# Layer B: one set of exponentials for two matrices, and 16x16 instead of 8x8 base blocks solved on VectorE

## What is computed

```python
    gc = jnp.cumsum(to_chunks(g, C, N), axis=-1)
    diff = gc[..., :, None] - gc[..., None, :]
    decay = jnp.where(tri, jnp.exp(jnp.where(tri, diff, 0.0)), 0.0)
    kb = kc * bc[..., None]
    lmat = jnp.where(strict, jnp.einsum('nbhik,nbhjk->nbhij', kb, kc) * decay, 0.0)
    rhs = jnp.concatenate([vc * bc[..., None], kb * jnp.exp(gc)[..., None]], axis=-1)
    sol = lax.linalg.triangular_solve(lmat, rhs, left_side=True, lower=True, unit_diagonal=True)
    u, w = sol[..., :dv], sol[..., dv:]
    aqk = jnp.einsum('nbhik,nbhjk->nbhij', qc, kc) * decay
    def step(S, xs):
        v_new = u_i - jnp.einsum('bhck,bhkv->bhcv', w_i, S)
        o_i = jnp.einsum('bhck,bhkv->bhcv', qg_i, S) + jnp.einsum('bhij,bhjv->bhiv', aqk_i, v_new)
        S = S * jnp.exp(gl_i)[..., None, None] + jnp.einsum('bhck,bhcv->bhkv', kdec_i, v_new)
```

## Time and profile before

| | us |
|---|---|
| median of three runs | 2143.05 |
| the three runs | 2143.21, 2138.21, 2143.05 |
| the profiled execution, whole | 2141.25 |
| its span, first to last instruction | 2139.2 |
| busy in the span: PE / DVE / ACT / POOL | 2098.6 / 954.5 / 711.9 / 449.6 |
| layer B's stage, on PE | 1062 to about 1701 |

### The profile page before, as it was taken

One profiled execution on the slowest core, in us unless ns is written; L12 is line 12 of the kernel. 1 busy time (PEld: TensorE's weight loads), 2 busy tenths in 40 slices (PEclk: granted clock), 3 DMA queues, 4 the chain that ended last, 5 costly groups with the idle time before them and its releaser, 6 DMA issues.

```text
span 2139.2 us, 39670 instructions
## 1 busy us (share of the span) xinstructions
PE 2098.6 (98%) x16046; PEld 1503.8 (70%) x16046; DVE 954.5 (45%) x2457; ACT 711.9 (33%) x1681; POOL 449.6 (21%) x640
## 2 busy tenths in 40 slices
PE   8999999999999999999999999999999999999998
PEld 6888888888888877555466676767766666665444
DVE  5234353354445445332255666666666233332252
ACT  4121311311231231221145555555555344542101
POOL 0522232231223214100033223322331200020000
PEclk9999999999999999999999999999999999999999
DMA  7511301211230137668212222222210361124451
GB/s 223 167 42 44 106 23 50 80 40 42 58 92 23 50 106 263 212 204 259 72 38 80 84 77 88 84 85 76 72 48 13 106 257 56 40 94 131 138 166 50
DMA packets 210251, 210.53 MB, mean 98 GB/s; under 512 B 14262, under 2 KB 181654, under 8 KB 209151
## 3 DMA queue, kind: packets, MB, share of 16 engines
q1 hardware_dynamic: 198070, 148.27, 23.4%
q0 software_dynamic: 12000, 59.73, 7.3%
HBM read 179.56 MB, written 68.23 MB: 116 GB/s over the span
## 4 chain that ended last, share of the span: by engine, by line
PE 48%; ACT 1%; DVE 1%; issue 0%; DVEq 0%
PE bank L2103 18%; PE bank L2913 8%; PE bank L3403 7%; PE bank L2161 5%; PE bank L2177 2%; PE bank L2159 2%; PE bank L2169 1%; PE bank L2929 1%; PE bank L2938 1%; PE bank L3381 1%; PE bank L3414 0%; PE bank L2192 0%; PE bank L3310 0%; PE bank L3287 0%; PE bank L2921 0%; PE bank L3297 0%
## 5 line engine op out<-in xcount | busy, mean ns | idle before, releaser
L887 PE MATMUL bank<-arena 128*128 128x256 f32 (+1 forms) x2688 | 631.7, 386 | 0.0
L887 PEld LDWEIGHTS bank<-arena 128*128 128x128 f32 x2688 | 494.5, 190 | 75.3
L2103 PE MATMUL bank<-arena 128*128 128x352 f32 x1296 | 457.7, 470 | 1.2 <-issue 1.1
L2103 PEld LDWEIGHTS bank<-arena 128*128 128x128 f32 x1296 | 217.9, 191 | 66.0 <-ACT arena L2338 0.6
L2913 PE MATMUL bank<-arena 128*128 128x352 f32 x576 | 176.4, 459 | 0.0
L3403 PE MATMUL bank<-arena 128*128 128x512 f32 x360 | 167.5, 599 | 0.0
L2161 PEld LDWEIGHTS bank<-arena 128*128 128x128 f32 x864 | 127.6, 194 | 44.2 <-DVE arena L2648 4.1
L2913 PEld LDWEIGHTS bank<-arena 128*128 128x128 f32 x576 | 106.6, 190 | 53.3
L1341 POOL TENSOR_TENSOR arena<-arena 128x272 f32<-128x272 f32 (+1 forms) x48 | 31.5, 656 | 507.7 <-ACT arena L1061 487.8
L2161 PE MATMUL bank<-arena 128*128 128x128 f32 x864 | 133.3, 280 | 4.0 <-DVE arena L2648 3.1
L1323 POOL TENSOR_TENSOR arena<-arena 128x512 f32<-128x512 f32 x96 | 122.7, 1278 | 11.1 <-POOL arena L1323 0.9
(11 more groups left out here) (433 smaller groups left out, 2800.4 us busy)
## 6 DMA issues: line engine op xcount, KB each, us to landing
arena<-in_w_in_a SPq DMA_DIRECT2D x48, 512.0 KB, 5.1
arena<-in_w_in_b SPq DMA_DIRECT2D x40, 512.0 KB, 6.6
arena<-in_cache_win_k SPq DMA_DIRECT2D x48, 256.0 KB, 6.1
arena<-in_cache_win_v SPq DMA_DIRECT2D x48, 256.0 KB, 4.8
out<-arena SPq DMA_DIRECT2D x40, 256.0 KB, 3.4
arena<-in_w_mem_kv SPq DMA_DIRECT2D x16, 512.0 KB, 8.1
arena<-in_cache_mem_k SPq DMA_DIRECT2D x32, 256.0 KB, 4.4
arena<-in_cache_mem_v SPq DMA_DIRECT2D x32, 256.0 KB, 4.2
```

The source lines that it names most:

```text
L887: m = nc.tensor.matmul(o[:, 0:hi - lo], w, y, start=k == 0 and i in (0, 1, 3, 5), stop=k == KH - 1, skip_group_check=i in (2, 4, 6))
L2103: m = nc.tensor.matmul(bank[j % 3][:, 0:PART], ring.slots[:, (B1 + b) % RING, k, :], part_in(k, part_), start=k == 0, stop=k == KD - 1)
```

## The change

Three things change.

1. A diagonal similarity. Row scaling by beta and by k's inverse norm on both sides is replaced by one column scaling, beta times the squared inverse norm, which is put in the exponent's bias. Then lmat and aqk hold the same exponentials: `ra` is broadcast and exponentiated once per group and multiplied with `kk` into LT and with `qk` into AT. `rl` and four of eight Exp go. The factors that come with v, k and the state change to suit (v times k's norm, k decayed times beta and the squared inverse norm); `factors` has four small DVE instructions with one wait on itself in place of three.
2. BASE is 16. Level 3 (x3, z3) goes from PE and DVE; DVE does 15 steps in place of 7 on 2 x 15 down to 2 x 1 entries per chunk (8 x j elements a partition in place of 16 x j), and the spreading transpose has 1920 columns in place of 896. `base_rows` waits for POOL's spread of the group before.
3. The slots: `ra` 5, `kt` 7, `kk` 8, `qk` 9, exps 7, choice 9, `base_rows` 11; steps 1, 1, 2, 1 in 12 to 15 and 2, 2, 1, 2, 1, 2 in 0 to 5; the norms in 1 to 5; x4 stays in slot 6. AT gets three buffers, LT two, in the spare branch rows of the last head.

The core of the diff (renamings of slices, `head_terms` and the prelude's three lines left out):

```diff
-FIRST_LEVEL = 3
+FIRST_LEVEL = 4
 BASE = 1 << FIRST_LEVEL
...
-    PREP = {6: ("kt",), 9: ("ra", "rl"), 11: ("qk", "kk"), 15: ("vt",)}
-    NEXT = ("rl", "kk")
-    LEVEL_SLOTS = {(3, "x"): 4, (3, "z"): 5, (4, "x"): 6, (4, "z"): 7, (5, "x"): 10, (5, "z"): 12, (6, "x"): 13, (6, "z"): 14}
-    AT_ROWS = 13
-    STEPS_BEFORE = {14: 1, 15: 1}
-    STEPS = {0: 1, 1: 2, 2: 1, 3: 1}
+    PREP = {5: ("ra",), 7: ("kt",), 8: ("kk",), 9: ("qk",), 15: ("vt",)}
+    NEXT = ("ra", "kk", "qk")
+    LEVEL_SLOTS = {(4, "x"): 6, (4, "z"): 7, (5, "x"): 10, (5, "z"): 12, (6, "x"): 13, (6, "z"): 14}
+    AT_ROWS = 11
+    STEPS_BEFORE = {12: 1, 13: 1, 14: 2, 15: 1}
+    STEPS = {0: 2, 1: 2, 2: 1, 3: 2, 4: 1, 5: 2}
...
-    AT_EXPS, AT_CHOICE = 9, 11
-    AT_SS, AT_ROOTS, AT_INV, AT_LOGS, AT_FACTORS, AT_OT = 3, 4, 5, 6, 7, 8
+    AT_EXPS, AT_CHOICE = 7, 9
+    AT_SS, AT_ROOTS, AT_INV, AT_LOGS, AT_FACTORS, AT_OT = 1, 2, 3, 4, 5, 8
...
-    TAP_AT = {0: 0, 4: 1, 11: 2}
-    conv_at = {1: (0, 1), 3: (0, 2), 4: (0, 3), 5: (1, 1), 7: (1, 2), 8: (1, 3), 12: (2, 1), 14: (2, 2), 15: (2, 3)}
+    TAP_AT = {0: 0, 6: 1, 11: 2}
+    conv_at = {1: (0, 1), 3: (0, 2), 4: (0, 3), 7: (1, 1), 9: (1, 2), 10: (1, 3), 12: (2, 1), 13: (2, 2), 15: (2, 3)}
...
-        def exps(G, name, buf, lo):
+        def exps(G):
...
-            readout(act, G, name)
+            readout(act, G, "ra")
+            act.wait_ge(hdv, 3 * G + 2)
             for n, c in enumerate(range(*GR[G % 2])):
-                i = nc.scalar.activation(buf[:, lo + n, :], buf[:, lo + n, :], ACT.Exp,
+                i = nc.scalar.activation(ATs[G % 3][:, n, :], ATs[G % 3][:, n, :], ACT.Exp,
                                          bias=hd[:, G // 2 % 2, BI, c:c + 1])
...
-            nc.vector.tensor_tensor(w[:, BI:RW + 1, :], w[:, LK:LK + 1, :].to_broadcast([P, 2, 4]), both_of(to_logs),
-                                    ALU.add).then_inc(hdv, 1)
-            nc.vector.tensor_tensor(w[:, NC_:KD_ + 1, :], w[:, RK:RK + 1, :].to_broadcast([P, 2, 4]),
-                                    both_of(to_roots), ALU.mult)
+            nc.vector.scalar_tensor_tensor(out=w[:, BI, :], in0=w[:, LK, :], scalar=2.0, in1=f(to_logs),
+                                           op0=ALU.mult, op1=ALU.add).then_inc(hdv, 1)
+            own(nc.vector.tensor_tensor(w[:, KD_, :], w[:, RK, :], w[:, RK, :], ALU.mult))
+            nc.vector.tensor_tensor(w[:, KD_, :], w[:, KD_, :], f(to_decays), ALU.mult)
             nc.vector.tensor_scalar(w[:, RQ, :], w[:, RQ, :], SCALE, None, ALU.mult).then_inc(hdv, 1)
...
-            if name == "rl":
-                nc.vector.tensor_tensor(lt, bk(b), wide4(mat(M_GT)), ALU.add).then_inc(rd_dve, 1)
-            elif name == "ra":
-                nc.vector.tensor_tensor(AT[:, cs, :], bk(b), wide4(mat(M_GE)), ALU.add).then_inc(rd_dve, 1)
+            if name == "ra":
+                nc.vector.tensor_tensor(at_, bk(b), wide4(mat(M_GE)), ALU.add).then_inc(rd_dve, 1)
             elif name == "kk":
-                dve.wait_ge(exd, 2 * G + 1)
-                nc.vector.tensor_tensor(lt, lt, bk(b), ALU.mult).then_inc(rd_dve, 1)
+                dve.wait_ge(exd, G + 1)
+                nc.vector.tensor_tensor(lt, at_, bk(b), ALU.mult).then_inc(rd_dve, 1)
...
             dve.wait_ge(chosen, 4 * (G + 1))
+            if G:
+                dve.wait_ge(spread, G)
```

More of the change, by code:

```diff
@@ L1905, in build @@
     spread_rows = upper[:, 2176:2176 + 4 * (BASE - 1) * 32]
-    LTs = [LT, upper[:, 3072:3584].rearrange("p (c e) -> p c e", e=P)]
-    to_logs, to_roots = (v.rearrange("p (t n) -> p t n", t=2)
-                         for v in (upper[:, 3584:3584 + 128], sb[:, small_at + 384:small_at + 512]))
+    spare = brT[:, HB - 1, 0:1024].rearrange("p (i c e) -> p i c e", i=2, e=P)
+    LTs = [LT, spare[:, 0]]
+    ATs = [AT[:, 0:4, :], AT[:, 4:8, :], spare[:, 1]]
+    to_logs, to_decays, minus_eg = (sb[:, small_at + 304 + 64 * i:small_at + 368 + 64 * i] for i in range(3))
     junk_s, junk_p = take(P), take(1)
@@ L1979, in build @@
     reader_of = lambda n: "act" if n == "ss" or n[:2] in ("qs", "tr") else "dve"
-    work = [(0, "ss"), (0, "rl"), (0, "kk")]
+    work = [(0, "ss"), (0, "ra"), (0, "kk"), (0, "qk")]
     for G in range(NG_ + 1):
@@ L2021, in build @@
     hcols = lambda v, h: v[:, h:64:HB]
-    RQ, RK, LK, NC_, KD_, BI, RW, SO = range(8)
+    RQ, RK, LK, QN, KN, KD_, BI, SO = range(8)
     def sides(v, k, b):
@@ L2211, in chunk_step @@
                 readout(pe, g, f"tr{c}")
-                to(g, f"av{c}", [(AT[:, c, :], vn[:, c % 2, :])])
+                to(g, f"av{c}", [(ATs[g % 3][:, cl, :], vn[:, c % 2, :])])
                 to(g, f"su{c}", [(kdec[:, c, :], vn[:, c % 2, :])])
@@ L2284, in _ @@
             unit(*u)
-        turned(0, "rl")
+        turned(0, "ra")
         for u in units[PER_HEAD + KD:PER_HEAD + 2 * KD]:
@@ L2288, in _ @@
         turned(0, "kk")
+        turned(0, "qk")
         for u in units[PER_HEAD + 2 * KD:PER_HEAD + AHEAD]:
@@ L2445, in _ @@
         silu(1, 0)
-        exps(0, "rl", LT, 0)
+        exps(0)
         piece(*second)
@@ L2463, in _ @@
                     chunk_step(G - 1, s)
[L2464 to L2467, removed]
+                if s == AT_EXPS and G + 1 < NG_:
+                    exps(G + 1)
                 if G == NG_ and s == 15:
@@ L2514, in norm_inverses @@
             h, cs = group(g)
-            w = hd[:, h % 2, RQ:RQ + 2, cs]
+            w = hd[:, h % 2, :, cs]
             readout(dve, g, "ss")
-            nc.vector.reciprocal(w, w).then_inc(hdv, 1)
+            nc.vector.reciprocal(w[:, RQ:RK + 1, :], w[:, QN:KN + 1, :]).then_inc(hdv, 1)
         def factors(g):
@@ L2522, in factors @@
             w = hd[:, h % 2, :, cs]
[L2523 removed]
+            f = lambda v: hcols(v, h)[:, cs]
             dve.wait_ge(hda, g + 1)
             dve.wait_ge(hdv, 3 * g + 1)
[L2526 to L2529 removed]
+            nc.vector.scalar_tensor_tensor(out=w[:, BI, :], in0=w[:, LK, :], scalar=2.0, in1=f(to_logs),
+                                           op0=ALU.mult, op1=ALU.add).then_inc(hdv, 1)
+            own(nc.vector.tensor_tensor(w[:, KD_, :], w[:, RK, :], w[:, RK, :], ALU.mult))
+            nc.vector.tensor_tensor(w[:, KD_, :], w[:, KD_, :], f(to_decays), ALU.mult)
             nc.vector.tensor_scalar(w[:, RQ, :], w[:, RQ, :], SCALE, None, ALU.mult).then_inc(hdv, 1)
         def head_terms():
[L2534 to L2538 removed]
+            nc.vector.tensor_tensor(to_logs, lbeta[:, 0:64], gc[:, 0:64], ALU.subtract)
+            nc.vector.tensor_tensor(to_decays, beta[:, 0:64], ekd[:, 0:64], ALU.mult)
+            own(nc.vector.tensor_scalar(minus_eg, eg[:, 0:64], -1.0, None, ALU.mult))
         def out_factors(g):
```

18 lines of the change are left out of this document (6 added, 12 removed).

## The result

| | median us | runs, lowest to highest |
|---|---|---|
| before | 2140.55 | 9, 2137.25 to 2143.26 |
| after | 2147.21 | 9, 2145.33 to 2149.24 |

The ratio is 1.0032, with a 95% interval of 1.0023 to 1.0041: the changed kernel is 6.7 us slower, and the prediction of 2137 missed by 10, with the wrong sign. The time lies within the range of 2118 to 2154. The profiled execution took 2148.14 us, its span is 2146.2. The page's busy times follow (us, share of the span, instructions): PE is busy 21.3 us less than before, and its share of the span fell from 98 to 97%.

What follows compares the result with a forecast made beforehand. PE, busy 98% of the span, was taken as the bound: 31.4 us gross gain less 26.7 (waits 21.5, start 2.2, end 3) made 4.7 faster, given as 2137. The range of 8 in 10 ran from 2118 to 2154.

Steps and rivals of the forecast that it cites:

- What PE loses, 1.89 a group: PE's list per group: z3 0.86, x3 0.57 and four `rl` transposes 0.46 go; times 16 is 30.2 us.
- DVE's durations: Step pairs at 0.0017 an element and 0.41 fixed, spread of 1920 columns 2.16; DVE carries 4.2 us more a group.
- x4's wait, 1.3: PE in slot 6 waits 1.3 us a group for DVE's factors, last two steps and transpose; bounds 0.9 and 2.0.
- x6's wait, 0.35: PE in slot 13 waits 0.35 us a group for DVE's spread and z5's readouts; bounds 0 and 0.8.
- DVE's free time between slot 14 and slot 2 takes up the rest: DVE has 1 to 2 us to spare before slot 2's readouts; POOL can take it away.
- Start and end, 2.2 and 3: Losses: 2.2 us at the start for the first base blocks, 3 from group 13 on, where DVE's chain sets the time.
- Rival A: DVE's chain is shorter than counted, x4 waits 0.4 at most: 21 us gain, 2120; chance 0.22.
- Rival B: x4's wait is 1.6 and half the groups drop PE's clock, decisive from about 1.5 on: 2153; chance 0.20.
- this trace agrees for the longer of its waits: In the kernel before, PE's clock fell after a wait of 1.54 us and stayed up after 1.37.
- Rival C: Each wait is 0.4 longer, POOL holding DVE in slot 5 or ACT late; no clock falls: 2142; chance 0.15.
- D: DVE is late in all slots from 11 to 5, steps costing more than the line; 1 us a group, 2150; chance 0.07.
- their own rule: No change lies between 2136.6 and 2149.5; forecast half faster: faster 0.42, no change 0.36, slower 0.22.

Runs made afterwards that it cites:

- e6: Changed kernel with the norms' sums behind slot 1's chunk product, last two steps in slot 4, slot 10's conv in slot 12: 2113.03 us, ratio 0.9866.
- e9: e6 with four projection units moved from the very end of the stage into slots 12 to 15 of group 13: 2108.86 us, ratio 0.9854.
- e4: Kernel before with the similarity (shared exponentials) alone, keeping BASE 8, level 3 and its slots: 2134.54 us, ratio 0.9981.
- e5: Kernel before with 16x16 base blocks alone, keeping both sets of exponentials and the norms in slots 3 to 7: 2138.85 us, ratio 0.9993.
- e1: Changed kernel with PE's column sums of the norms (ss) put behind slot 1's chunk product (tr): 2136.21 us, ratio 0.9976.
- e8: Kernel before with only the norms' slots moved, from 3 to 7 to 1 to 5: 2150.05 us, ratio 1.0051.
- e2: Changed kernel with the last two base steps and the turning transpose moved from slot 5 to slot 4 on DVE: 2123.35 us, ratio 0.9923.
- e3: Changed kernel with the edits of both e1 and e2: 2114.50 us, ratio 0.9875.
- e6_again: The kernel of e6 run once more on the same chip as e9: 2111.75 us, ratio 0.9866.

## Why the prediction was wrong, step by step

- **What PE loses, 1.89 a group: right.** With hardly a wait left (e6, e9) the period is 34.04, 1.87 under the 35.91 of before without its single gap. e4 shows 0.39 to 0.49 for the 0.46 of `rl`, and e5 agrees with the 1.43 of level 3 within 0.1. The prelude's wait of 1.19 is gone in the changed kernel. `to_blocks` has 2560 rows, the PE transposes 256.
- **DVE's durations: right.** The spread of 1920 columns takes 2.17 (2.16 forecast), and the pairs are as the line had them.
- **x4's wait, 1.3: right**, with about 1.15 and 1.31 by turns and 1.22 in the mean, in all of groups 1 to 12. The working holds too. The two chains into `factors` do end together: Ln at 1234.64, the masking at 1234.56, `factors` begins at 1234.67; and the four instructions take 0.5.
- **x6's wait, 0.35: right**, 0.25.
- **"DVE's free time between slot 14 and slot 2 takes up the rest": the step that failed.** It put PE's waits outside x4 and x6 at nothing. The move of the norms from slots 3 to 7 to slots 1 to 5 was given no price. Only DVE's queue was looked at there, and POOL's hold on it. What had to be followed was each wait of PE whose count includes the moved `ss`. That wait costs 0.55 in its bracket and 0.26 around it, 0.81 a group by e1's period, 11.0 us in the time by e1 and 10.0 by e8. The sum came out 4.7 faster; with this term it is 6.3 slower, and 6.7 was measured. That the two lie 0.4 apart is in part luck, since the runs of either kernel spread over 4 to 6 us.
- **Start and end, 2.2 and 3: about right in sum.** e1, which has them both, comes within 1 us of the forecast, though not cleanly: in its profiled execution the clock over 1060 to 1070 is 0.69, and 1.00 in that of the kernel before. At the start x4 waited 1.76, and the clock fell behind it, which the 2.2 had no term for: to the next x4 it is 34.30 us there and 31.54 in e2, and the next x4's wait of 1.21 leaves some 1.5 of that for the clock. Group 13 to 14 has waits of 1.83, 2.02, 1.28, 1.53 and 1.74 where before had 1.54, 1.6 and 1.9. The two parts were not measured one by one.
- **Rival A** (no wait): x4 did wait. e2 and e3 show what A would have been; its 2120 is near e2's 2123 by luck, since e2 had the third wait still, and without that e3 takes 2114.5.
- **Rival B** (the clock): the repeated waits, 1.14 to 1.33, left the clock up, as B had it for waits under 1.5. The granted clock over the 4 us from where the columns say (us, busy of PE, PEld, DVE, ACT, POOL, clock, DMA share, GB/s) is 0.61 after the wait of 1.76 at 1129.66, 1.00 after 1.31 at 1236.47, and 0.59 after 1.83 at 1600.55. Over the 6 us behind x4 it is 1.00 in every one of groups 1 to 12. In the profiled execution the clock fell at the two ends only.

```profile
1131.00:1135.00 4.00, 4.00 (x74) 2.71 (x74) 1.64 (x3) 0.67 (x3) 0.61 (x1) 0.61 0.15 65
1236.50:1240.50 4.00, 4.00 (x111) 3.09 (x112) 2.08 (x6) 2.20 (x4) 0.37 (x2) 1.00 0.16 68
1601.00:1605.00 4.00, 4.00 (x75) 3.01 (x76) 2.00 (x6) 3.19 (x7) 0.14 (x1) 0.59 0.01 4
```

  But the border of about 1.5 was read from too few waits. The trace of the kernel before has a wait of 1.59 ahead of 1617.34 with the clock at 1.00 behind it, so "this trace agrees for the longer of its waits" was read wrongly; the changed kernel has one of 1.74 ahead of 1633.48, also with 1.00. In e1 the clock fell to 0.61 behind a wait of 1.33. The window of the kernel before, then e1's wait and the window behind it:

```profile
1617.50:1621.50 4.00, 4.00 (x110) 2.65 (x110) 2.79 (x13) 2.63 (x7) 0.00 (x0) 1.00 0.00 0
```
```profile
1611.13 0.46 PE L2162 MATMUL bank<-arena 128*128 128x128 f32 x2 [1.33 <-DVE arena L2643]
```
```profile
1611.50:1615.50 4.00, 4.00 (x74) 2.98 (x74) 2.69 (x14) 2.49 (x6) 0.05 (x1) 0.61 0.02 4
```

  So the length of one wait does not settle whether the clock falls. The Trainium skill (TensorE: Matmul & The Clock Gate, HAM oscillation) tells of a kernel whose longer wait in each round has PE begin every round at half clock. Of the 12 middle rounds of this kernel, each with a wait of 1.1 to 1.3, none shows it.
- **Rival C** (both waits longer, POOL or a late ACT): neither wait was longer. In slot 3, behind the third wait, a conv took 2.11 in place of 0.74 beside POOL's product (below). In slot 5, `factors` to the end of the transpose takes 1.74 with POOL's small sample instructions beside it (before 1236.47) and 1.58 without them (before 1272.87). That difference of 0.16 is the whole of x4's 1.31 and 1.15 by turns, within the 0.3 that the prediction had left for it. **D** (DVE late in all slots): no; with its last two steps moved (e2) PE waits for DVE in a middle group 0.25 at x6 and nowhere else.

The chances do not follow from their own rule either: B two thirds and D half slower make 0.17, not 0.22, and C, the other half of the forecast and what is left of B and D make some 0.43 for no change, not 0.36.

Open: how much of the 2.9 between e9 and e6_again comes from the four units; whether e6 is faster than e3 in the time; what the gap of 1.12 in the kernel before is; why the clock falls behind some waits and not behind others as long; and whether POOL's instruction held DVE's in e5, which rests on durations that end together and was not tested by moving POOL's.

## What to carry to other kernels

When an engine signals through a count, each wait names not an instruction but all that is numbered up to it: after a move, compare the order of the numbers with the order in which the engine does them, for every reader of the count, even if the moved work is 0.25 us on an idle engine. A slot's cost is read from what stands behind the waiting instruction, and a chain of small steps is best ended a slot before its user: the same 15 steps cost 1.22 us of waiting a group at the end of slot 5 and nothing at the end of slot 4. And if a forecast sums the waits at two places, list PE's other waits on the moved engines and show for each why it is early.

## What the runs showed of the hardware

- A conv of DVE took 1.37 us longer when it lay beside POOL's product of 512 elements (1230.98 to 1232.03) than a slot later. That the one held the other was not tested. The Trainium skill (GPSIMD Engine Reference, section 1, Specifications) has the SBUF interfaces shared with VectorE, with contention for DVE instructions that have two SBUF inputs, as a conv has; by that rule the trace agrees. DVE and POOL of the changed kernel:

```profile
1230.48 2.11 DVE L2499 SCALAR_TENSOR_TENSOR arena<-arena 128x512 f32<-128x512 f32 x1
...
1233.22 0.74 DVE L2499 SCALAR_TENSOR_TENSOR arena<-arena 128x512 f32<-128x512 f32 x1
```
```profile
1230.98 1.05 POOL L2814 TENSOR_TENSOR arena<-arena 128x512 f32<-128x512 f32 x1
```

- PE's clock stayed up through waits of 1.14 to 1.33 us in twelve groups in a row, and fell to the lower level of 1.2 GHz for a few us after single ones of 1.54, 1.76 and 1.83. After others of 1.59 (before) and 1.74 (after) it stayed up, and after one of 1.33 (e1) it fell.
- A block transpose of DVE costs 1.04 ns for each further column, over a factor of 15 in width: 0.31 us for 128 columns, 2.17 for 1920.
